# Route part of a hybrid encoder kernel: gate products behind the scores, one comparison for both one-hots, up to eight gathered rows on the way

## What is computed

```python
gates = jax.nn.sigmoid(gate_cols + b_gate).reshape(bsz, seq, N_BRANCH, D_MODEL)
y = gates[:, :, 0] * (branches[0] @ w_branch[0])
...
q = (xb @ w_q).reshape(P_TOKEN_BLOCK, P_HEADS, 2, P_HALF)
s = jnp.einsum('thcd,ckd->thck', q, sub_keys).astype(jnp.float32)
sv, si = lax.top_k(s, P_TOPK)
...
top_s, top_pos = lax.top_k(cand, P_TOPK)
g = jax.nn.softmax(top_s, axis=-1).reshape(P_TOKEN_BLOCK, P_HEADS * P_TOPK)
u = u_tab[experts]
vv = v_tab[experts]
a = jax.nn.gelu(jnp.einsum('td,ted->te', xb, u), approximate=False) * g
return jnp.einsum('te,ted->td', a.astype(vv.dtype), vv)
```

## Time and profile before

| what | before |
|---|---|
| median of 3 runs | 4460.01 us (4444.33 to 4460.23) |
| the profiled execution | 4453.37 us, its span 4451.4 us |
| granted TensorE clock of the profiled execution, mean | 0.954 |
| TensorE busy | 3973.7 us (89%) |
| VectorE busy | 2640.4 us (59%) |
| ScalarE busy | 1511.7 us (34%) |
| GpSimd busy | 1276.2 us (29%) |
| HBM read, written | 788.87 MB, 115.34 MB |

### The profile page before, as it was taken

The page is one execution under the profiler, slowest core; times in us unless marked ns, Lnnn a source line. Parts: engine busy times, 40 slices in busy tenths (PEclk is TensorE's granted clock), DMA queues, the critical chain, the costliest instruction groups (busy, mean ns, idle before and its releaser), DMA issues.

```text
span 4451.4 us, 61311 instructions
## 1 busy us (share of the span) xinstructions
PE 3973.7 (89%) x18070; PEld 2992.1 (67%) x18070; DVE 2640.4 (59%) x5662; ACT 1511.7 (34%) x2428; POOL 1276.2 (29%) x884
## 2 busy tenths in 40 slices
PE   5888999799998989999869889997999988899998
PEld 2334455399998987777624344653999888777776
DVE  3443323246997957777634432331579988577776
ACT  3224333233443333333332333432334433333332
POOL 0000000046865652222100000000468655422221
PEclk9898999999999999999989899998999999999999
DMA  4341112134788899998634311122357888888885
GB/s 167 114 146 44 56 50 93 69 136 162 262 299 306 339 334 328 327 335 319 217 117 149 104 50 54 62 90 76 136 186 257 315 301 323 323 323 318 321 323 217
DMA packets 340821, 906.71 MB, mean 204 GB/s; under 512 B 28688, under 2 KB 160016, under 8 KB 337168
## 3 DMA queue, kind: packets, MB, share of 16 engines
q1 hardware_dynamic: 215824, 497.43, 31.7%
q0 software_dynamic: 84480, 306.22, 18.6%
q10 hardware_dynamic: 40320, 100.68, 5.9%
HBM read 788.87 MB, written 115.34 MB: 203 GB/s over the span
## 4 chain that ended last, share of the span: by engine, by line
PE 44%; DMA 17%; issue 15%; DVE 15%; POOL 4%; ACT 3%; DVEq 1%; POOLq 0%; SPq 0%; ACTq 0%; PEldq 0%
DMA W<-tab_v 14%; PE bank L683 13%; PE bank L753 7%; PE bank L672 4%; PE bank L674 4%; PE bank L673 4%; DVE u_lo L1950 3%; PE bank L809 2%; PE bank L780 2%; POOL gathered_rows L1431 2%; DMA gathered_rows<-u_rows,arena 2%; PE bank L739 1%; DVE gathered_rows L1820 1%; DVE arena L1860 1%; PE bank L723 1%
## 5 line engine op out<-in xcount | busy, mean ns | idle before, releaser
L1423 POOL TENSOR_TENSOR u_lo<-W,u_hi 128x1024 fp32r<-128x1024 f32 x272 | 688.7, 2533 | 1154.2 <-ACT u_hi L1256 1152.1
L672 PE MATMUL bank<-h_hi,u_hi 128*128 128x384 f32 (+1 forms) x2176 | 765.9, 352 | 48.5 <-POOL u_lo L1423 46.1
L673 PE MATMUL bank<-h_lo,u_hi 128*128 128x384 f32 (+1 forms) x2176 | 744.8, 342 | 0.0
L674 PE MATMUL bank<-h_hi,u_lo 128*128 128x384 f32 (+1 forms) x2176 | 744.6, 342 | 0.0
L672 PE MATMUL bank<-u_hi,a_hi 128*128 128x512 f32 x1536 | 608.7, 396 | 74.3 <-DVE a_lo L1954 74.1
L674 PE MATMUL bank<-u_hi,a_lo 128*128 128x512 f32 x1536 | 604.3, 393 | 0.0
L673 PE MATMUL bank<-u_lo,a_hi 128*128 128x512 f32 x1536 | 604.3, 393 | 0.0
L1339 ACT ACTIVATE u_hi<-W 128x1024 fp32r<-128x1024 f32 x256 | 272.5, 1064 | 756.3 <-DMA W<-tab_v 388.2
L672 PEld LDWEIGHTS bank<-h_hi,u_hi 128*128 128x128 f32 x2176 | 417.3, 192 | 59.7 <-issue 37.0
L673 PEld LDWEIGHTS bank<-h_lo,u_hi 128*128 128x128 f32 x2176 | 417.2, 192 | 5.4
L674 PEld LDWEIGHTS bank<-h_hi,u_lo 128*128 128x128 f32 x2176 | 415.3, 191 | 5.4
(11 more groups left out here) (191 smaller groups left out, 5774.5 us busy)
## 6 DMA issues: line engine op xcount, KB each, us to landing
W<-tab_u SPq DMA_DIRECT2D x256, 512.0 KB, 3.7
W<-tab_v SPq DMA_DIRECT2D x256, 512.0 KB, 9.5
W<-stream SPq DMA_DIRECT2D x206, 512.0 KB, 3.7
act_scratch<-act_out ACTq DMA_DIRECT2D x256, 192.0 KB
route_scratch<-arena ACTq DMA_DIRECT2D x24, 2048.0 KB, 11.1
act_in<-act_scratch SPq DMA_DIRECT2D x64, 768.0 KB, 5.7
g_cur<-route_scratch SPq DMA_DIRECT2D x64, 768.0 KB, 10.2
gate_raw<-gate_tiles POOLq DMA_DIRECT2D x48, 512.0 KB, 4.1
```

The source lines that it names most:

```text
L672: mm(out, w[0], a[0], start=first, stop=False)
L673: mm(out, w[0], a[1], start=False, stop=False)
L674: return mm(out, w[1], a[0], start=False, stop=last)
L1423: nc.gpsimd.tensor_tensor(u_parts[1][:, b, :], raw, u_parts[0][:, b, :].bitcast(F32), ALU.subtract).then_inc(col_lo.sem, 1)
```

## The change

In `attention`, the gate products of a unit stand directly behind its scores, ahead of the transposes, outputs and preparation. In the route part, one comparison writes both one-hots of a quad (1024 elements per partition instead of 512), and a multiplication by the shares, 512 elements, comes behind the quad's `sparse_up`; the shares are first copied into free columns of the PSUM bank that holds the row of numbers 0 to 127. The gathers go by the table GATHERED: up to column c, as many as the quads up to column c need and four more, at most four behind one column.

```diff
--- before.py
+++ after.py
@@ -311,6 +311,7 @@
 
         at[0] = shared
         route = [carve(128 * TOKENS, [128, TOKENS]) for _ in range(2)]
+        onehots = arena[:, at[0]:at[0] + 4096].rearrange("p (s b t i) -> p s b t i", s=2, b=4, t=4)
         cand = carve(HEADS * 256, [HEADS, 256])
         onehot16 = carve(HEADS * 256, [HEADS * 16, 16])
         pickT = carve(3 * DENSE, [3, DENSE])
@@ -444,7 +445,12 @@
             QUADS[n] = list(range(first, first + width))
             first += width
         assert first == Q, first
+        GATHERED, ahead = [], 24 + 4
+        for c in range(2 * COLUMNS["route"] + COLUMNS["rest"]):
+            ahead += len(QUADS[c % COLUMNS["route"]]) if c < 2 * COLUMNS["route"] else 2
+            GATHERED.append(min(ahead, SPARSE + 6))
         iota_placed = sem("iota_placed")
+        shares_placed = sem("shares_placed")
         onehots_i = signal("onehots_i", {"route": Q})
         onehots_g = signal("onehots_g", {"route": Q})
         route_product = signal("route_product", {"route": Q})
@@ -813,6 +819,9 @@
                 for u in range(len(units) + 3):
                     if u < len(units):
                         scores(u)
+                    if stage in GATE_WORK:
+                        for i, k in gate_products(stage, u):
+                            gate_product(stage, layer, step, i, k, bool(beside))
                     if 2 <= u <= len(units) + 1:
                         turn(u - 2)
                         if stage == "swa":
@@ -821,9 +830,6 @@
                         output(u - 3)
                     for part in [p for after, p in beside if after == u]:
                         part()
-                    if stage in GATE_WORK:
-                        for i, k in gate_products(stage, u):
-                            gate_product(stage, layer, step, i, k, bool(beside))
                     if stage == "swa" and u == 0 and not beside:
 
                         load_wait("swa", layer, step, 0)
@@ -1451,10 +1457,11 @@
                                 lower("route", c // COLUMNS["route"], c % COLUMNS["route"])
                             else:
                                 lower("rest", 0, c - 2 * COLUMNS["route"])
-                            for _ in range(4 if c == 0 else 2):
-                                if upcoming < SPARSE + 6:
-                                    gather(upcoming)
-                                    upcoming += 1
+                            issued = 0
+                            while upcoming < GATHERED[c] and issued < 4:
+                                gather(upcoming)
+                                upcoming += 1
+                                issued += 1
                         assert upcoming == SPARSE + 6
                         for j in range(KEYS):
                             if upcoming < 2 * SPARSE:
@@ -1888,6 +1895,11 @@
                     for step in range(1, TT):
                         select(step, step - 1 if step > 1 else None, range(8 * (step - 1), 8 * step))
                     dve.wait_ge(iota_placed, layer + 1)
+                    dve.wait_ge(picks_copied.sem, picks_copied.at("picked", layer, 1, 1))
+                    dve.sem_inc(held, 1)
+                    shares = PS[3][:, 128:512]
+                    nc.vector.tensor_copy(shares[:, 0:256], pickT[:, 2, 0:256]).then_inc(shares_placed, 1)
+                    dve.wait_ge(shares_placed, layer * 2 + 1)
                     dve.sem_inc(held, 1)
 
                     for step in range(2):
@@ -1896,20 +1908,22 @@
                                 copy_picks(TT - 1)
                                 dve.wait_ge(picks_copied.sem, picks_copied.at("picked", layer, 2, 1))
                                 dve.sem_inc(held, 1)
-                            elif step == 0 and q == 0:
-                                dve.wait_ge(picks_copied.sem, picks_copied.at("picked", layer, 1, 1))
+                                nc.vector.tensor_copy(shares[:, 256:384], pickT[:, 2, 256:384]).then_inc(shares_placed, 1)
+                                dve.wait_ge(shares_placed, layer * 2 + 2)
                                 dve.sem_inc(held, 1)
 
                             dve.wait_ge(route_product.sem, route_product.at("route", layer, step, q - 3))
                             four = step * (DENSE // 2) + 4 * q
                             iota = PS[3][:, 0:128]
-                            tt(oh_i[:, q % 4], pickT[:, 0, four:four + 4].unsqueeze(2).broadcast_to([128, 4, 128]),
-                               iota.unsqueeze(1).broadcast_to([128, 4, 128]), ALU.is_equal).then_inc(onehots_i.sem, 1)
-                            for t in range(4):
-                                last = ts(oh_g[:, q % 4, t, :], iota, pickT[:, 1, four + t:four + t + 1],
-                                          pickT[:, 2, four + t:four + t + 1], ALU.is_equal, ALU.mult)
-                            last.then_inc(onehots_g.sem, 1)
+                            tt(onehots[:, :, q % 4],
+                               pickT[:, 0:2, four:four + 4].unsqueeze(3).broadcast_to([128, 2, 4, 128]),
+                               iota.unsqueeze(1).unsqueeze(1).broadcast_to([128, 2, 4, 128]), ALU.is_equal
+                               ).then_inc(onehots_i.sem, 1)
                             sparse_up(24 + Q * step + q)
+                            dve.wait_ge(onehots_i.sem, onehots_i.at("route", layer, step, q + 1))
+                            tt(oh_g[:, q % 4], oh_g[:, q % 4],
+                               shares[:, four:four + 4].unsqueeze(2).broadcast_to([128, 4, 128]), ALU.mult
+                               ).then_inc(onehots_g.sem, 1)
                     for k in range(24 + 2 * Q, SPARSE):
                         sparse_up(k)
                     dve.wait_ge(row_used.sem, row_used.at("late", layer, 0, 8))
```

## The result

The changed kernel takes 4322.31 us (median of 4 runs, 4317.14 to 4331.88), the kernel before 4452.17 beside it (4 runs, 4442.16 to 4460.23): a ratio of 0.9712, with a 95% interval of 0.9679 to 0.9745. A second comparison later gave 0.9706 [0.9693, 0.9719]. The forecast was 4380 with a range of 4345 to 4426: the sign was right, and the effect, 127 us between the two profiled executions (4453.4 and 4326.75), is well over the 72 us of the sum.

A forecast was written before the change was run, and what follows sets the result against it. No sole bound in the route part: TensorE, VectorE and DMA floors lie within 2%, with about 50 us of waits a layer. 4453.4 - 66 (route part) - 6 (gates) = 4381, said as 4380 us; range 4345 to 4426.

The forecast's parts named there:

- the sum: Whole kernel: 66 us from the route part and 6 us from the gate products off 4453.4, giving 4381 us.
- Rival (1): Route part: the stores take over and all 48 us are back, 4447 us; chance 0.11 together with rival (4).
- Rival (2): Route part: the row transfers queue and half of the waits remain, 4414 us; chance 0.13.
- Rival (3): Route part: the multiplication runs at L1860's price, a quad takes 3.72 us, 4478 us in all; chance 0.06.
- Rival (4): Route part: GpSimd waits for buffers at a gather and holds up `lower`, so TensorE waits there; 0.11 with (1).
- What is late next: Route part: DMA work of 289 us at a share of 0.93 leaves 311 and 308 us, a gain of 66.
- Hidden: Route part: with four buffers VectorE is up to three quads (9 us) ahead, so TensorE doesn't see the later one-hot.
- One-hots: Route part, VectorE: a quad takes 2.89 us, 0.13 less, saving 6 us a pass of VectorE's time.
- Gates behind scores: Both attentions: moving the gate products gains 6 us together, with bounds of -5 and 14.
- the 0.65: Window attention: gates between scores and sums let ScalarE's table load start 0.65 us earlier, 6 x 0.65 = 3.9 us.
- The latent terms: Latent attention: 0.75 wait gone, 2.06 stays, 1.30 becomes 2.06, the last costing 6 x 0.76 = 4.6 us.
- the ring's wait: Route part, column 22: gathers fall behind use, lead 2 rows at a pass's start, -2 behind column 19.

The follow-up runs named there:

- the quarter stores: Stores and read-back of routes cut from 2 MB to 512 KB a block: changed kernel 4315.02 us, 0.9703; kernel before 4407.21 us, 0.9904.
- the gates between: Changed kernel with the gate products between the turning of the probabilities and the output, in both attentions: 4329.3 us, 0.9737.

## Why the prediction was wrong

**The sign, the mechanism and VectorE's quad: right.** Rows came late because the loop gathered two rows where three were used, and late rows cost TensorE's waits and, behind them, its clock. The price list held: comparison 1.22 (1.21 said), product 0.69 (0.68), clock 0.98, row waits in the quads near nothing, route part 302 us at a share of 0.95. Rival (1), the stores take over, is out by the quarter stores: they cost the changed kernel 7 us in all. Rival (2) is out by the 2.7 us of waits left. Rival (3), the dear multiplication, didn't come; a product with both inputs in SBUF is dearer (1.25 us on average), but by meeting GpSimd's residuals and not by the price of L1860. Rival (4) is out: GpSimd's longest wait before a gather is 1.0 us until 1540.

**"What is late next" failed by 0.02 in the share, and in what it meant.** The text took a DMA share of 0.93 as the new bound: 311 and 308 us, a gain of 66. The share came out at 0.95, with 0.99 over 140 us without any idle TensorE, and the part at 302 and 301. The bound was never DMA: with the share pushed down to 0.87 the part shortened by 3.5 us only. With the row waits gone, TensorE's own floor of 285 us, its remaining waits and some lower clock set the time. By the start of the last eight columns (1600.58 and 3819.56 before, 1549.04 and 3702.84 after) the part went from 340.1 and 348.9 us to 300.4 in both layers. Taking 0.97, the rows' own best, would have given 298 and 295, too low by 2 and 5; the right way was to add up what is left for TensorE. The text had that sum: 48 us of waits and clock a layer, 96 in all, and the cap by the share cut it to 66. Route and rest part gained just 96. Part of that match is luck, since the 48 count 5.2 us that stayed. The Trainium skill's figure of about 358 GB/s (DMA: Bandwidth & Descriptors, "Where 436 GB/s comes from"), which the text had already set aside, is passed in this case: 367 over the part, 385 over 140 us, part of it stores.

**"Hidden" for the faster quad failed.** *One-hots* costed 6 us a pass of VectorE's time and put none of it in the sum. Behind the table it gave 5 to 6 us a layer (20 us between the medians of the two kernels, 0.983 and 0.9788). It rested on four one-hot buffers hiding VectorE. With the table and the old quad they don't quite: TensorE waits for one-hots 12 times, 6.3 us in the first layer, and with the faster quad still 4 times, 2.7 us, so VectorE's beat shows through. The same sentence, that the finished one-hot comes later but "TensorE doesn't see it once rows are there", held only with its condition: without the table that later place costs 59 us.

**"Gates behind scores" was mis-sized: 6 us said, 34 to 37 measured, and the ends of -5 and 14 didn't hold it.** A step of the window attention lost 3.85 us where the sum had 0.65 + 0.37. The step that failed is the 0.65: it let ScalarE's chain start where the sums end, so that only the 0.65 us between that end and the table load could be won. From the scores of unit 1 on, the way to the rotation is (before first; its sums and rotation are in the earlier trace rows, its table load in the earlier trace rows):

```profile
196.17 0.70 PE L780 MATMUL bank<-arena 64*128 64x256 f32 x2
```

```profile
235.29 0.70 PE L786 MATMUL bank<-arena 64*128 64x256 f32 x2
...
236.04 1.88 PE L759 MATMUL bank<-hT,gate_raw 128*128 128x512 f32 x4
237.76 1.02 PE L729 MATMUL bank<-arena,C 128*128 128x512 f32 x2
...
239.46 1.88 PE L759 MATMUL bank<-hT,gate_raw 128*128 128x512 f32 x4
...
242.56 1.12 PE L737 MATMUL bank<-arena,C 128*128 128x512 f32 x2 [1.11 <-DVE arena L1518]
```

```profile
237.72 1.28 ACT L1125 ACT_TABLE_LOAD   x1
```

The table load doesn't wait for the sums: in the changed kernel it starts at 237.72, and the sums only at 237.76. It follows unit 1's scores by 2.4 us in both kernels, and the rotation follows them by 7.27 (7.26 with the gates between), so the chain runs from those scores and is as long as before. But TensorE now has two groups of four gate products to do in these 7.27 us where it had one, and a group takes 1.72: the wait went from 2.82 to 1.11, by 1.71. The turn's 0.37 went too, and a wait of 0.60 for a copy of gate products (`mixT`) came.

TensorE's busy time fell by 2.5 us, which the term had not looked for at all. From start to next start the 48 gate products of a step take 23.9 us before and 21.2 after. Of the difference 1.6 us is clock: behind the wait of 2.82 us four of them took 3.47 us, at the lower of the two levels, where 1.88 is usual; behind 1.11 us the level stays. The other 1.1 us are the neighbours of 64 that the groups no longer have on both sides. The latent terms were wrong in detail and nearly nothing in sum: the second sums still wait 1.30 us (2.06 was said), the first 1.92, the turn's 0.75 is gone, and the clock from 320 to 540 us reads 0.90 where it was 0.91.

The stretch ahead of the route part, read in fourteen executions, agrees with the medians. With the gates in their old place (six executions, two layers each) it is 1260.4 to 1267.0 us long, 1264.3 on average, and in the new one (eight executions) 1245.4 to 1249.9, 1248.0 on average: 16 us a layer, 33 in all. The 12 and 17 us of the two executions above are within this spread.

**The wait of the earlier trace rows was put at the wrong column and down to the wrong thing.** The earlier trace rows were read as column 22 of the first pass and the ring's wait, and TensorE's 5.2 us for the low half counted among what goes. Between the last quad and that wait TensorE runs 48 matmuls without a quad, which are columns 22 and 23. So the column that waits, and the `lower` ahead of the late gather, is the first of the second pass, where the lead is two rows again. The ring's own waits are those as in the earlier trace rows; by the order of the buffers the row behind that one was asked for at 1387.62 and used at 1398.76, late in issue and 11 us on its way. The wait for the low half is still there in the changed kernel, 5.29 us at 1403.41, again behind 48 matmuls. ScalarE's and GpSimd's timelines of the changed kernel show the chain:

```profile
1391.76 0.34 ACTq L1278 DMA_DIRECT2D act_scratch<-act_out  x1
1398.51 1.28 ACT L1262 ACT_TABLE_LOAD   x1 [6.92 <-issue]
1399.81 1.06 ACT L1262 ACTIVATE u_hi<-W 128x1024 fp32r<-128x1024 f32 x1
```

```profile
1400.94 2.34 POOL L1429 TENSOR_TENSOR u_lo<-W,u_hi 128x1024 fp32r<-128x1024 f32 x1 [11.94 <-ACT u_hi L1262]
```

ScalarE stands for 6.92 us waiting for nothing that the profile shows, exactly where its loop over the two passes goes back to its start, and the high half, the low half and TensorE's column follow from it. The kernel before has the same gap (6.8 us) there. That the loop's jump is the cause is only argued: a kernel with the two passes written out on ScalarE wasn't tried.

In numbers: the two parts that the sum had at 66 and 6 gave 92 and 35. 26 us are missing in the first and 29 in the second; together they are the 55 us between 72 and 127. By the stretches the first is 96, so 30 are missing: 18 by the assumed DMA bound (311 + 308 against 300.4 twice), 8 in the rest part (43.3 and 42.0 us before, 38.7 and 39.1 after), which the sum left at nothing without a reason, and 4 because the second layer's part was 349 us long and not 345.

What stays open: how the gates' gain splits between idle time, neighbours and clock in other stretches than the step shown, and what makes ScalarE stand at the start of the second pass.

## What to carry to other kernels

A resource near full is a bound only if somebody waits for it: before capping a gain by its share, look for waits that end on it, and add up what remains on the critical engine instead. Ask of each wait on TensorE what the clock does behind it and which instruction stands ahead of it, because a stage's gain lay as much in busy time (44.9 to 42.4 us) as in idle time. Count what stands between the instruction that starts a chain and the one that waits for its end, on both sides: here the chain kept its 7.27 us and one more group of products moved in under it. And the parts of a change are not additive: the faster one-hots lose 59 us alone and win 20 behind the table, since an operation was moved behind one that could be late.

## What the runs showed of the hardware

- A VectorE product of 512 elements takes 0.68 to 0.705 us with an input in PSUM, in all 192 cases, and up to 2.85 us with both inputs in SBUF when it meets a GpSimd residual of 2.4 us. A residual that starts just behind such a product took 2.87.
- A dependent VectorE instruction starts 1.26 us behind a comparison whose independent neighbour starts 1.13 behind it: 0.13 us, hidden by one instruction put between.
- TensorE's granted clock stayed at 1.00 over steps with idle times of 1.11 us, and read 0.96 over steps with one of 2.82 us.
- Four 128x128x512 products take 1.72 us between neighbours of 128*128, 1.82 with one neighbour that has a side of 64 (64*128 or 128*64), 1.91 with two.
- The DMA engines moved 385 GB/s for 140 us, reads and stores together, while TensorE never stood idle.
- Fewer bytes per store, 512 KB instead of 2 MB, cut the waits for gathered rows in the kernel before by a third (57.4 to 38.3 us in the first layer), and gained 7 us in all where the rows had a lead.
